# Expert routing by one-hot products, token rows gathered turn by turn

## The reference, cut to what matters

```
expert = g_sel[:, None] * EXPERTS_PER_GROUP + top_i          # two experts for each token
order = argsort(expert)                                       # assignments sorted by expert,
dest = p_start[e_s] + arange(2 n) - start[e_s]                # each expert padded to whole blocks
tok_buf[dest] = t_s;  w_buf[dest] = w_s
y = (silu(xb @ w1[e]) * (xb @ w3[e])) @ w2[e]                 # block by block, xb = h[tok]
out = zeros.at[tok_buf].add(y * w_buf)
```

## Time and profile before

| | |
|---|---|
| median of 3 runs | 3871.69 us |
| profiled execution | 3865.83 us |
| its span | 3864.0 us |
| mean granted clock of TensorE | 0.896 |
| PE, DVE, ACT, POOL busy | 85%, 44%, 20%, 3% of the span |
| moved by DMA | 601.41 MB, mean 156 GB/s |

### The profile page before, as it was taken

How to read it: one execution, slowest core, us unless ns; L and a number is a source line. 1 busy time by engine, 2 the same in 40 slices (tenths; PEclk the granted TensorE clock), 3 DMA queues, 4 the chain that set the end, 5 groups by cost and what they waited for, 6 DMA issues and landing times.

```text
span 3864.0 us, 47136 instructions
## 1 busy us (share of the span) xinstructions
PE 3268.1 (85%) x15310; PEld 2093.4 (54%) x15310; DVE 1686.8 (44%) x2497; ACT 773.1 (20%) x1822; POOL 121.5 (3%) x131
## 2 busy tenths in 40 slices
PE   6999787789896599999679997878898946999994
PEld 3666555566543355555346664556665424555552
DVE  4777624454424223232367775244543241232324
ACT  2222223342111011111122221233321100111111
POOL 2100000000000100000100000000000010000002
PEclk9999998787697799999879998977887978999997
DMA  9500100000100899999810001000001019999996
GB/s 268 141 22 11 39 7 12 6 7 12 44 3 1 350 411 406 411 409 415 306 32 22 22 11 40 6 12 6 7 12 47 0 56 368 410 408 413 409 410 254
DMA packets 138921, 601.41 MB, mean 156 GB/s; under 512 B 13545, under 2 KB 47849, under 8 KB 121385
## 3 DMA queue, kind: packets, MB, share of 16 engines
q1 hardware_dynamic: 103320, 483.31, 31.7%
q0 software_dynamic: 16944, 60.89, 4.9%
q10 hardware_dynamic: 18528, 55.59, 3.9%
HBM read 524.97 MB, written 74.78 MB: 155 GB/s over the span
## 4 chain that ended last, share of the span: by engine, by line
PE 76%; DVE 8%; issue 6%; DMA 4%; ACT 3%; POOL 2%; ACTq 1%; DVEq 1%; SPq 0%; POOLq 0%; PEldq 0%
PE ps L1054 7%; PE ps L1250 7%; PE ps L1351 6%; PE ps L1451 6%; PE ps L1441 6%; PE ps L1410 5%; PE ps L1095 5%; PE ps L1416 5%; PE ps L1188 4%; PE ps L1265 3%; PE ps L1468 3%; PE ps L1315 3%; PE ps L1150 3%; PE ps L1175 3%; DMA arena<-xg 2%
## 5 line engine op out<-in xcount | busy, mean ns | idle before, releaser
L1095 PE MATMUL ps<-arena 128*128 128x260 f32 x1024 | 288.9, 417 | 12.6 <-ACT arena L763 9.9
L1688 DVE TENSOR_REDUCE negmax<-ps 16x1 f32<-16x16 f32 (+8 forms) x216 | 151.4, 704 | 324.6 <-PE ps L1155 323.4
L1054 PE MATMUL ps<-arena 128*128 128x512 f32 (+1 forms) x768 | 262.4, 500 | 5.4 <-DVEq L553 3.2
L763 ACT ACTIVATE arena<-ps,negmax 16x16 f32<-16x16 f32 (+8 forms) x216 | 150.9, 699 | 512.5 <-DVE negmax L1688 494.7
L1250 PE MATMUL ps<-arena 128*128 128x256 f32 (+1 forms) x1152 | 251.6, 380 | 0.0
L1351 PE MATMUL ps<-arena 128*128 128x512 f32 (+1 forms) x576 | 250.3, 592 | 0.0
L1410 PE MATMUL ps<-arena 128*128 128x512 f32 x544 | 247.2, 608 | 2.6 <-ACT arena L976 2.6
L1451 PE MATMUL ps<-arena 128*64 128x256 f32 x2176 | 242.3, 381 | 0.0
L1416 PE MATMUL ps<-arena 128*128 128x256 f32 x1088 | 240.4, 379 | 0.0
L1441 PE MATMUL ps<-arena 128*128 128x512 f32 x544 | 239.1, 592 | 0.0
L1416 PEld LDWEIGHTS ps<-arena 128*128 128x128 f32 x1088 | 206.7, 190 | 42.6 <-issue 16.3
(11 more groups left out here) (319 smaller groups left out, 4282.2 us busy)
## 6 DMA issues: line engine op xcount, KB each, us to landing
arena<-w SPq DMA_DIRECT2D x204, 2048.0 KB, 12.9
xg<-arena POOLq DMA_DIRECT2D x51, 512.0 KB, 12.3
arena<-xg ACTq DMA_DIRECT2D x38, 512.0 KB, 10.2
xg<-arena ACTq DMA_DIRECT2D x34, 512.0 KB, 7.4
arena<-w_in SPq DMA_DIRECT2D x16, 1024.0 KB, 5.7
arena<-xg ACTq DMA_DIRECT2D x34, 256.0 KB, 11.1
xg<-arena ACTq DMA_DIRECT2D x68, 128.0 KB, 9.3
arena<-w_in SPq DMA_DIRECT2D x16, 512.0 KB, 4.3
```

The source lines that it names most:

```text
L1054: mm = pe.matmul(dst[0:hi - lo, a:b], w[:, k, lo:hi], uT[:, k, a:b], start=(k == 0), stop=(k == KD - 1))
L1095: mm = pe.matmul(out, w_qk[b][:, k, :], uT[:, k, lo:hi], start=(k == 0), stop=(k == KD - 1), skip_group_check=True)
L1688: v.tensor_reduce(negmax[0:r, at:at + 1], flat[0:r, side:side + wide_], AX.X, ALU.max, negate=True)\
```

## The change

The normalised tokens are stored in token order to a new DRAM tensor `u_rows`, tile by tile, by SP during phase 4. The scatter is gone. After `dest`, VectorE splits each slot number into turn and place in the turn and builds one-hot matrices, `chosen` (place, 192 columns) and `token_in` (turn, 34 columns, times the token number). PE multiplies them, 18 products for each of the two block sizes, which gives in PSUM the token number of each slot: slots on partitions, turns in columns. VectorE copies them out as integers (`ids`). In phase 6 POOL takes the place of ACT for the token loads: for each block it copies one column of `ids` to `pick` and gathers the rows of `u_rows` with one indirect DMA. Slots without a token have number 0 and get token 0's row.

The expert table is worked out with slots on partitions (three comparisons, one sum), put on a diagonal and spread by one product with ones; it and `pairs` stand ahead of the slot numbers now, and so does `r_done`. The scratch tiles of the routing have moved out of the place of the weight buffers, and SP no longer waits in turn 0. The zero fill is still made, and waits for the first head's projections of the HGRN phase.

```diff
-        s = Place(SCRATCH + D)
+        s = Place(SCRATCH + 8 * D + KD * L)
+        lgT = s.take(L)
+        E = [s.take(T, EXPERTS), s.take(T, EXPERTS)]
+        both = s.take(T, EXPERTS)
+        assert s.at <= SCRATCH + 8 * D + KD * L + 2 * KD * P
+        s = Place(SCRATCH + 8 * D + KD * L + 2 * KD * P)
...
+        chosen = arena[:, s.at:s.at + 2 * T * SPAN].rearrange("p (m n) -> p m n", m=2 * T)
...
+        u_rows = nc.dram_tensor("u_rows", (L, D), F32, kind="Internal").ap()
...
+                    for j in range(T):
+                        wait_alone(sp, n_u[1], ONE + layer * T + j + 1)
+                        sp.dma_start(u_rows[cols(j), :], mix[0:rows(j), j, :]).then_inc(r_u, 16)
...
-                            if k == 0:
-                                wait_alone(sp, m_x[0], before * 16 + layer * 32 + 16)
                             wait_alone(sp, m_y[k], ONE + t)
                             sp.dma_start(W2[k], A["w2"][layer, e].rearrange("(j p) d -> p j d", p=P))\
...
-                    act.wait_ge(m_xt, ONE + turns)
-                    act.dma_start(xb[:, 0, :], xg[0:P, :]).then_inc(m_x[0], 16)
-                    act.wait_ge(m_xt, ONE + turns + 2)
-                    act.dma_start(xb[:, 0, :], xg[SPAN:SPAN + P, :]).then_inc(m_x[0], 16)
+                    act.wait_ge(m_xt, ONE + turns + 1)
...
-                        act.wait_ge(m_xt, ONE + turns - 2)
-                        act.dma_start(xb[0:SMALL, 1, :], xg[bass.ds(i * SPAN + P, SMALL), :]).then_inc(m_x[1], 16)
...
-                        act.wait_ge(m_xt, ONE + turns + 3)
-                        act.dma_start(xb[:, 0, :], xg[bass.ds((i + 2) * SPAN, P), :]).then_inc(m_x[0], 16)
...
+                    pe.wait_ge(r_diag, ONE + layer + 1)
+                    pe.matmul(ps[:, 3, 0:2 * ROUNDS], ones[:, :], diagonal.rearrange("p k i -> p (k i)"),
+                              start=True, stop=True).then_inc(r_table, 1)
+                    for k in range(2):
+                        pe.wait_ge(r_chosen, ONE + layer * 2 + k + 1)
+                        for m in range(k * T, (k + 1) * T):
+                            for bank, n, at in ((4, P, 0), (6, SMALL, P)):
+                                mm = pe.matmul(ps[0:n, bank, 0:ROUNDS + 2], chosen[:, m, at:at + n], token_in[:, m, :],
+                                               start=(m == 0), stop=(m == 2 * T - 1))
+                    mm.then_inc(r_named, 1)
...
-            wait_alone(pool, h_wfq, 16)
-            wait_alone(pool, h_wig, 16)
-            wait_alone(pool, s_par, 16 * 8)
+            wait_alone(pool, h_q, ONE + 1)
...
-                    wait_alone(pool, r_dest, ONE + layer + 1)
-                    for k in range(2):
-                        for j in range(T):
-                            pool.indirect_dma_start(
-                                out=xg[:, :], out_offset=bass.IndirectOffsetOnAxis(ap=dest[0:rows(j), k, j:j + 1], axis=0),
-                                in_=mix[0:rows(j), j, :], in_offset=None).then_inc(r_sc, 16)
-                    wait_alone(pool, r_sc, layer * 32 * T + 32 * T)
                     meet(pool, layer, 5)
                 if stop > 6:
+                    before = pool.value_load(pairs[0:1, 1:2], min_val=0, max_val=ROUNDS)
+                    count = pool.value_load(pairs[0:1, 0:1], min_val=1, max_val=ROUNDS)
+                    def fetch(k, i, nth):
+                        n = P if k == 0 else SMALL
+                        pool.tensor_copy(pick[0:n, k:k + 1], ids[k][0:n, bass.ds(i, 1)]).then_inc(m_pick, 1)
+                        wait_alone(pool, m_pick, ONE + nth)
+                        pool.indirect_dma_start(
+                            out=xb[0:n, k, :], out_offset=None, in_=u_rows[:, :],
+                            in_offset=bass.IndirectOffsetOnAxis(ap=pick[0:n, k:k + 1], axis=0)).then_inc(m_x[k], 16)
+                    turns, picks = before * 3 + 2 * layer, before * 2 + 2 * layer
+                    wait_alone(pool, r_u, (layer + 1) * 16 * T)
+                    fetch(0, 0, picks + 1)
+                    wait_alone(pool, m_xt, ONE + turns + 2)
+                    fetch(0, 1, picks + 2)
+                    with pool.Fori(0, count) as i:
+                        t = before + i
+                        turns, picks = t * 3 + 2 * layer + 2, t * 2 + 2 * layer + 2
+                        wait_alone(pool, m_xt, ONE + turns - 2)
+                        fetch(1, i, picks + 1)
+                        wait_alone(pool, m_xt, ONE + turns + 3)
+                        fetch(0, i + 2, picks + 2)
+                    wait_alone(pool, m_x[0], (before + count) * 16 + layer * 32 + 32)
...
+                    do(v.tensor_scalar(ends[:, 0, :], big_to, slot_no, None, ALU.is_le))
+                    do(v.tensor_scalar(ends[:, 1, :], small_to, slot_no, None, ALU.is_le))
+                    do(v.tensor_scalar(after, slot_no, bigs, rounds, ALU.subtract, ALU.add))
+                    do(v.tensor_scalar(ends[:, 2, :], small_to, after, None, ALU.is_le))
+                    do(v.tensor_reduce(experts_f, ends, AX.X, ALU.add))
+                    do(v.tensor_scalar(beyond, slot_no, bigs, None, ALU.is_ge))
+                    do(v.tensor_tensor(after, experts_f[:, 2:3], experts_f[:, 0:1], ALU.subtract))
+                    do(v.scalar_tensor_tensor(out=experts_f[:, 0:1], in0=after, scalar=beyond, in1=experts_f[:, 0:1],
+                                              op0=ALU.mult, op1=ALU.add))
+                    do(v.tensor_scalar(experts_f, experts_f, float(EXPERTS - 1), None, ALU.min))
+                    v.tensor_tensor(diagonal, ident[:, 0:ROUNDS].unsqueeze(1).to_broadcast([P, 2, ROUNDS]),
+                                    experts_f[:, 0:2].unsqueeze(2).to_broadcast([P, 2, ROUNDS]), ALU.mult)\
+                     .then_inc(r_diag, 1)
+                    do(v.tensor_tensor(pairs_f[:, 1:2], pairs_f[:, 0:1], pairs_f[:, 1:2], ALU.add))
+                    do(v.tensor_copy(pairs[:, 0:1], rounds[0:1]))
+                    do(v.tensor_copy(pairs_f[:, 0:1], rounds[0:1]))
+                    do(v.tensor_copy(pairs[:, 1:2], pairs_f[:, 1:2]))
...
+                    v.wait_ge(r_table, ONE + layer + 1)
+                    v.tensor_copy(blk_expert[:, :].rearrange("p (i k) -> p k i", k=2),
+                                  ps[0:1, 3, 0:2 * ROUNDS].rearrange("p (k i) -> p k i", k=2)).then_inc(r_done, 1)
...
-                    v.tensor_copy(dest[:, :, :], destf).then_inc(r_dest, 1)
-                    def expert_of(out, ends, number):
-                        do(v.tensor_tensor(cmp[0:1], ends[0:1].unsqueeze(1).to_broadcast([1, ROUNDS, EXPERTS]),
-                                           number[0:1].unsqueeze(2).to_broadcast([1, ROUNDS, EXPERTS]), ALU.is_le))
-                        do(v.tensor_reduce(out[0:1], cmp[0:1], AX.X, ALU.add))
...
-                    v.tensor_copy(pairs[:, 1:2], pairs_f[:, 1:2]).then_inc(r_done, 1)
-                    v.wait_ge(r_done, ONE + layer + 1)
+                    do(v.tensor_copy(dest[:, :, :], destf))
+                    do(v.tensor_scalar(dest_i, dest[:, :, :], 6, None, ALU.arith_shift_right))
+                    do(v.tensor_scalar(dest_i, dest_i, 171.0, None, ALU.mult))
+                    do(v.tensor_scalar(dest_i, dest_i, 9, None, ALU.arith_shift_right))
+                    do(v.tensor_copy(dest_turn, dest_i))
+                    do(v.scalar_tensor_tensor(out=dest_in, in0=dest_turn, scalar=-float(SPAN), in1=destf,
+                                              op0=ALU.mult, op1=ALU.add))
+                    v.wait_ge(r_u, (layer + 1) * 16 * T)
+                    for k in range(2):
+                        mine, shape = slice(k * T, (k + 1) * T), [P, T, ROUNDS + 2]
+                        do(v.tensor_tensor(token_in[:, mine, :], dest_turn[:, k, :].unsqueeze(2).to_broadcast(shape),
+                                           in_span[:, 0:ROUNDS + 2].unsqueeze(1).to_broadcast(shape), ALU.is_equal))
+                        do(v.tensor_tensor(token_in[:, mine, :], token_in[:, mine, :],
+                                           token_no.unsqueeze(2).to_broadcast(shape), ALU.mult))
+                        v.tensor_tensor(chosen[:, mine, :], dest_in[:, k, :].unsqueeze(2).to_broadcast([P, T, SPAN]),
+                                        in_span.unsqueeze(1).to_broadcast([P, T, SPAN]), ALU.is_equal)\
+                         .then_inc(r_chosen, 1)
+                    v.wait_ge(r_named, ONE + layer + 1)
+                    for k, n, bank in ((0, P, 4), (1, SMALL, 6)):
+                        v.tensor_copy(ids[k][0:n], ps[0:n, bank, 0:ROUNDS + 2]).then_inc(r_ids, 1)
+                    v.wait_ge(r_ids, ONE + layer * 2 + 2)
```

More of the change, by code:

```diff
@@ L396, in build @@
         first8 = s.take(PER_GROUP)
-        blk_no = s.take(ROUNDS)
+        route_c = s.take(SPAN + T + 1)
+        in_span, token_no, slot_no = route_c[:, 0:SPAN], route_c[:, SPAN:SPAN + T], route_c[:, SPAN + T:SPAN + T + 1]
```

(53 more changed lines are left out.)

1 line of the change is left out of this document (removed).

## The result

The changed kernel takes 3837.71 us, median of 5 runs (3832.99 to 3845.20), the kernel before 3869.14 in the same comparison; the ratio of the runs is 0.993, 95% interval 0.9901 to 0.9959. The forecast was 3841.0 in 3822 to 3857. The profiled execution has a span of 3843.4 us.

A forecast was written before the change was run, and what follows sets the result against it. PE (99.21 of 100 us busy) and the DMA queues (408 GB/s) both bound the expert loops, so gains come ahead of them: 2 x (11.6 + 3.75) = 30.7 us off 3871.69 gives 3841.0 us, range 3822 to 3857.

The forecast's parts named there:

- Expert table, weights early: Routing ahead of the loops: table work adds 3.5 us before `place`; SP's first weight load goes out 13.8 us earlier.
- VectorE's one-hot matrices: Routing after `dest`: two halves of 0.52, 0.52 and 1.96 us, 3.0 each, ready at 1261.35 and 1264.35.
- The series on PE: 36 two-pass products giving token numbers: 12.0 us, midway between 8.6 at the high clock and 15.3 at the low.
- Ids, barrier and POOL's copy: From products to first fetch issue: 0.5 us copies, 3.1 barrier and count, 0.5 POOL's copy (bounds nothing to 0.92).
- The landing: First token fetch, issued among turn 0's weight loads: takes 10.2 us; first product then 11.6 us earlier per layer.
- First turns: Early loop turns: the small set's waits of 4.0 and 3.5 us vanish, 3.75 us a layer, bounds 0 and 4.
- Steady turn, token-order copy, zero fill: Later loop turns, the 9 stores during output projection, and the delayed 51 fill stores: each changes the time by nothing.
- B: Rival, first fetch: not held up by weights, lands in 3.3 us; gain 44.5 us, 3827.2 us; chance 0.17.
- C: Rival, ahead of loops: low clock throughout, landing 13.25 us, early waits stay; gain 5.3 us a layer, 3861.1; chance 0.14.
- D: Rival, expert loops: small fetch late every turn, exceeding 15.5 us of room; 45 us slower, 3917 us; chance 0.07.
- The 1.1 us more: Loop fetches: each of two issues beside VectorE might take 1.1 us more, leaving 13.3 us of room.
- The sum of 30.7 us: Both layers' total gain: 2 x (11.6 + 3.75), from the earlier first product and the lost early waits.

The follow-up runs named there:

- r4: Changed kernel with the one-hot matrices in bfloat16 and the token number in two parts, 68 columns; median 3827.71 us, ratio 0.989.
- r6: Changed kernel with SP holding W2 and the small block's weights of turn 0 until the first token set landed; one run, 3847.40 us.
- r8: Kernel before, scatter kept, with routing scratch moved and SP's turn 0 wait removed, so all weights go out early; median 3898.27 us, ratio 1.0085.
- r2: Changed kernel with the zero fill put back behind its old, earlier waits; median 3836.99 us, ratio 0.9912.
- r1: Changed kernel run again with no edit; median 3836.99 us, ratio 0.9921.
- r5: Changed kernel with both the bfloat16 one-hot series and turn 0's last 8 MB of weights held until the first fetch landed; median 3819.34 us, ratio 0.9873.
- r7: Changed kernel with POOL asking for each small set only after PE finished the same turn's W1 product; one run, 3900.25 us.
- r3: Changed kernel with SP holding W2 and the small block's weights of turn 0 until the first token set landed; ratio 0.9923.

## Why the prediction was right

Measured times of layer 0 are put 9.3 us back, so that they stand in the clock of the earlier trace rows.

- *Expert table, weights early.* SP's first load went out at 1261.50, that is 1252.2; I had 1253.75. The last of turn 0's weights landed at 1294.65, that is 1285.3; I had about 1286.
- *VectorE's one-hot matrices.* 0.49, 0.49 and 1.97 us where I had 0.52, 0.52 and 1.96; PE started on the first half at 1261.3 (I had 1261.35).
- *The series on PE* is the term that was mis-sized: 16.88 us against 12.0, outside both my bounds (8.6 and 15.3). It ran at the low clock to its end, and a product with 64 weight columns cost nearly what one with 128 did, where I had let the row of 64-column transposes price it.
- *Ids, barrier and POOL's copy*: from the end of the series to the issue 3.3 us, I had 4.1. POOL's copy and its wait, the part without a row, took 1.05 us from 1289.73 to 1290.78, above the 0.5 that I took and above its bound of 0.92; the barrier took less than the old one.
- *The landing* is the second mis-sized term, 5.12 us against 10.2, and it is tied to the first. The queues were done with the weights at 1294.7, so the fetch, asked for 4.0 us later than I had it, met only their end. r4 shows the price that I had used (9.84 us) as soon as the series is short. The two errors, +4.9 and -5.1 us, cancel, and my sum did not know that they would: it priced the two apart. That the first product came at 1289.6, where I had 1290.9, is in this part luck; 12.9 and 13.6 us were gained, I had 11.6.
- *First turns*: 4.3 and 4.7 us, I had 3.75. The waits that went are 4.0 and 3.5 us; the rest, within 0.1 to 0.3 us, is the first product, 0.4 and 0.9 us shorter. I had named two causes, the 8 MB landed by then and POOL asking some 4 us sooner. Both are there, and either takes most: with POOL early and the 8 MB held the waits of the second to fourth turn do not return (r6), and with the 8 MB early and ACT late 0.8 and 1.3 us of them stay (r8). POOL asks 14.9 us ahead of the transposes in the loop (1369.38, they start at 1384.26), where ACT asked 11.4 us ahead (1342.21, they would have started at 1353.6).
- *Steady turn, token-order copy, zero fill*: nothing, as forecast. For the fill r2 shows it. For the copy r8, which has none, serves: from the first product of the output projection to the router's first it takes 146.2 and 146.0 us, and r1, with the copy, 146.1 and 146.1.

Of the rivals, B's landing nearly came, 5.12 us here and 4.96 in r1 where I had named under 5 as its sign, but not for its reason, for the weights were nearly in. Beside the weights the fetch took 9.84 us (r4), and beside idle queues 4.5 (r5), not 3.3. C had its long series, more than the 15 us that I had named as its sign, but neither its landing nor its early waits. Its other sign, a first turn above 36 us, says nothing: the first turn is 36.5 us here by the low clock alone. D did not happen: there is no wait at L1440 in this profile. But it was nearer than I had worked out. The room was 14.9 us and not 15.5, and the small set took 13.4 to 14.8 of it, not 11.1; its price per turn is lower (r7). The 1.1 us more that I allowed for each issue beside VectorE did not come, for the 72 issues took 0.92 to 1.04 us. The one row that I had it from, 2.02 us, was a single one: the first scatter (0.92) and the third to sixth (0.96, 1.20, 0.95, 0.95) were issued beside VectorE's work as well.

The sum of 30.7 us stands against 35.5 in the profiles and 31 between the medians; the interval of the ratio leaves 16 to 38.

What stays open: which clock or wait makes the attention phases differ by some 15 us between executions, and why the clock rises up to 1.5 us sooner or later in the first product of the loop. Not tried were the earlier expert table without the gather, and leaving out the zero fill altogether.

## What to carry to other kernels

Where every engine waits for a scatter before a loop that then needs its own loads, store the rows once in order and gather them where they are used; but early loads alone made this kernel slower (r8), since they delayed the transfer that all waited for. With the gather, holding them back made no difference to the whole time that the runs could tell (r3). When two steps in a row lead to one landing, price them together: here shortening the products by 10 us gave 4, until the loads in the way were held back as well. Measure such a change by a distance inside the profile that the noise of other phases does not enter, and repeat the profile: this distance moved by 2 us without an edit. Before a load is handed to another engine, set its landing against the time from the request to the need: here up to 14.8 of 14.9 us were used, and asking after one more product cost twice the gain (r7).

## What the runs showed of the hardware that I had not expected

The mean times of the series by shape, in the changed kernel from 1268 to 1290 us:

```profile
L1396 PE MATMUL ps<-arena 128*128 128x34 f32 x36 | 11.6, 416 | 14.5 <-DVE arena L2179 14.5
L1396 PE MATMUL ps<-arena 128*64 128x34 f32 x36 | 7.7, 310 | 0.0
```

The times of one overlap; 72 passes in 16.88 us are 0.234 each. If the 128-column ones took the 0.247 of the transposes, the 64-column ones took 0.22, not half. In bfloat16 36 passes with 68 columns took 6.77 us, 0.188 each, at the same clock. And a gather of 512 KB by POOL beside idle queues took 4.5 us from its issue where ACT's plain load took 3.3 (r5), while beside the weights both took about 10 (9.84 in r4; 10.2 for ACT's loads in the loop). The small set of 256 KB, asked for 2 us behind the big one, landed in 13.4 to 14.8 us in the changed loop; asked for 11 us behind it, in 6.8 to 8.2 (r7).
